# Layer-norm sums summed whole before TensorE, weight splits moved ahead of the first reads, and other orders in attention and the output projection

## The reference, cut to what matters

```
def rmsnorm(x, g):
    return x * rsqrt(mean(x * x, axis=-1) + eps) * g

def conv_ffn(x, g, w_up, conv_w, conv_b, w_down):
    u = rmsnorm(x, g) @ w_up                      # 1024 -> 2 * 2816
    c = conv_b + sum(conv_w[j] * shifted(u, j) for j in range(3))
    gate, val = split(c, 2)
    return (silu(gate) * val) @ w_down

for i in range(2):
    h = rmsnorm(x, attn_norm[i])
    y_mix = rwkv7_time_mix(...) if i == 0 else dilated_attention(q, k_sh, v_sh)
    y_mem = memory_attention(...)
    x = x + concat(y_mix, y_mem) @ w_out[i]
    x = x + conv_ffn(x, ffn_norm[i], ...)
```

## Time and profile before

| | us |
|---|---|
| time, median of 3 runs (lowest to highest) | 1308.78 (1308.62 to 1309.12) |
| the profiled execution's own time | 1308.9 |
| its span, first to last instruction | 1307.0 |
| busy: PE, DVE, ACT, POOL | 1275.2, 992.2, 646.0, 321.3 |

### The profile page before, as it was taken

How to read it: one execution, slowest core, us unless ns; L and a number is a source line. 1 busy time by engine, 2 the same in 40 slices (tenths; PEclk the granted TensorE clock), 3 DMA queues, 4 the chain that set the end, 5 groups by cost and what they waited for, 6 DMA issues and landing times.

```text
span 1307.0 us, 27113 instructions
## 1 busy us (share of the span) xinstructions
PE 1275.2 (98%) x10688; PEld 1041.3 (80%) x10688; DVE 992.2 (76%) x1486; ACT 646.0 (49%) x1068; POOL 321.3 (25%) x302
## 2 busy tenths in 40 slices
PE   7999999999999999999999999999999999999999
PEld 5876777776578888988889988776778889888898
DVE  4777777787468889857889958548578899578896
ACT  6575645563244445334546555547554453344542
POOL 3369777784420000000001256330100000000000
PEclk9999999999999999999999999999999999999999
DMA  8100111114023332233332342211133323333331
GB/s 326 49 22 32 55 55 40 55 32 168 18 97 97 96 108 90 86 104 96 96 105 90 112 143 81 65 49 33 33 98 97 96 89 122 97 96 98 119 109 46
DMA packets 30055, 114.35 MB, mean 87 GB/s; under 512 B 3456, under 2 KB 5248, under 8 KB 29184
## 3 DMA queue, kind: packets, MB, share of 16 engines
q1 hardware_dynamic: 29952, 112.89, 26.0%
HBM read 110.78 MB, written 2.10 MB: 86 GB/s over the span
## 4 chain that ended last, share of the span: by engine, by line
PE 86%; DVE 5%; ACT 3%; issue 1%; POOL 0%; DVEq 0%; POOLq 0%; ACTq 0%
PE bank L665 84%; PE bank L1384 1%; DVE arena L2132 1%; ACT arena L1581 1%; PE bank L971 0%; DVE sin_part L2696 0%; DVE cos_part L2723 0%; DVE in_lo L2143 0%; PE bank L1266 0%; DVE head_stat L2706 0%; ACT w_hi L1464 0%; DVE w_lo L2118 0%; PE bank L1289 0%; DVE stat L2210 0%; DVE cos_part L2692 0%
## 5 line engine op out<-in xcount | busy, mean ns | idle before, releaser
L665 PE MATMUL bank<-in_hi,w_hi 128*128 128x512 f32 x704 | 274.9, 390 | 0.9 <-DVE in_lo L2143 0.9
L665 PE MATMUL bank<-in_lo,w_hi 128*128 128x512 f32 x704 | 273.9, 389 | 0.0
L665 PE MATMUL bank<-in_hi,w_lo 128*128 128x512 f32 x704 | 273.9, 389 | 0.0
L1464 ACT ACTIVATE w_hi<-ring 128x1024 fp32r<-128x1024 f32 (+2 forms) x176 | 161.4, 919 | 205.2 <-PE bank L665 204.9
L665 PE MATMUL bank<-z,w_hi 128*128 128x256 f32 (+1 forms) x1088 | 221.9, 303 | 0.7 <-DVE w_lo L2118 0.7
L665 PEld LDWEIGHTS bank<-z,w_hi 128*128 128x128 f32 x1088 | 175.9, 191 | 9.7 <-DVE w_lo L2118 0.9
L2118 DVE TENSOR_TENSOR w_lo<-ring,w_hi 128x1024 fp32r<-128x1024 f32 (+2 forms) x156 | 161.1, 1035 | 26.4 <-ACT w_hi L1464 25.0
L665 PE MATMUL bank<-z,w_lo 128*128 128x256 f32 (+1 forms) x544 | 164.1, 302 | 0.0
L665 PEld LDWEIGHTS bank<-in_hi,w_hi 128*128 128x128 f32 x704 | 132.2, 188 | 29.6 <-DVE in_lo L2143 1.3
L665 PEld LDWEIGHTS bank<-in_lo,w_hi 128*128 128x128 f32 x704 | 132.2, 188 | 27.7 <-issue 0.5
L665 PEld LDWEIGHTS bank<-in_hi,w_lo 128*128 128x128 f32 x704 | 132.1, 188 | 27.4
(11 more groups left out here) (292 smaller groups left out, 2239.3 us busy)
## 6 DMA issues: line engine op xcount, KB each, us to landing
ring<-w_ring SPq DMA_DIRECT2D x119, 512.0 KB, 3.5
ring<-w_ring SPq DMA_DIRECT2D x32, 704.0 KB, 4.1
ring<-w_pairs SPq DMA_DIRECT2D x18, 512.0 KB, 3.9
arena<-w_mem SPq DMA_DIRECT2D x2, 2048.0 KB, 19.0
arena<-w_ring SPq DMA_DIRECT2D x4, 512.0 KB, 4.9
x<-xT SPq DMA_DIRECT2D x1, 2048.0 KB, 8.5
outT<-x SPq DMA_DIRECT2D x8, 256.0 KB, 2.0
mask<-masks SPq DMA_DIRECT2D x1, 1536.0 KB, 7.0
```

The lines of the kernel that those rows point to most:

```text
L665: return nc.tensor.matmul(out, lhsT, rhs, start=first, stop=last, skip_group_check=True)
L1464: return nc.scalar.activation(out, in_, ACT.Copy)
```

## The change

1. **Squares summed whole.** The sum now takes in slice 7 as well, and TensorE makes one matmul against the ones, not two. In MLP 0 POOL still adds (7 additions, not 6), and the matmul stands before slice 2 of product 1. In MLP 1 the 7 additions are DVE's, behind the split of product 1's weights, and the matmul stands before slice 7 of product 1. `squares_summed(q, n)` counts the additions.
2. **Splits ahead of reads.** In pair 0 of each MLP's first half, the split of product 3's weights stands ahead of the read of product 0 on DVE, and ahead of the first own tap on ACT.
3. **Projection of layer 1.** `turn_heads` stands one slot later in steps 9 and 13; ACT does the exponentials 6 of the memory attention ahead of the turned heads 13.
4. **Attention.** In step 0 DVE takes over one of ACT's two `pT` copies, and ACT does the exponentials 1 ahead of its other copy. In step 2 DVE's `pT` copy stands behind both halves of `masked`; in step 5 `masked` and the bound stand ahead of the normalisation. On PE, `out_b_memory(0)` stands ahead of `outputs(5)`.
5. **Output projection of layer 1.** ACT makes the high copy of attention slice 0 before it copies the last output; the weight splits stand between ACT's `in_hi` of even slices and their square.

```diff
+        def squares_summed(q, n):
+            return (0, KD - 1, 2 * KD - 3)[q] + n
...
             def square_sum(q):
-                pe.wait_ge(sem("sq_sum"), (KD - 2) * (q + 1))
-                mm(bank[7][:, :], ones, y[:, 0, :], True, False)
-                pe.wait_ge(sem("xsq"), KD * (q + 2))
-                mm(bank[7][:, :], ones, y[:, KD - 1, :], False, True).then_inc(sem("x_ss"), 1)
+                pe.wait_ge(sem("sq_sum"), squares_summed(q, KD - 1))
+                mm(bank[7][:, :], ones, y[:, 0, :]).then_inc(sem("x_ss"), 1)
...
-                            if half == 0 and q == 0 and s == 1:
-                                square_sum(2 * l)
+                            sum_at = (2, KD - 1)[l] if half == 0 and q == 0 and s == 1 else None
...
                             split_product(bank[b][:, :], n, in_hi, in_lo, KD,
+                                          between=lambda k: square_sum(2 * l) if k == sum_at else None,
...
-                if slot == 1 and 5 <= s <= 16:
+                if slot == (2 if s in (9, 13) else 1) and 5 <= s <= 16:
                     turn_heads(s - 5)
...
-            outputs(last - 2)
             pe.wait_ge(sem("da_sm"), 2 * 2 * RES)
             out_b_memory(0)
+            outputs(last - 2)
             weights(last - 1)
...
# ACT, squares()
-                    due = (slots == 1 or m % 2 == 1) and n >= N_SPLIT + 2
-                    if due:
+                    if slots == 1 and n >= N_SPLIT + 2:
                         split(n)
                     act.wait_ge(sem("x_up"), KD * e + m + 1)
                     gained_high((G_FFN0, G_FFN1)[e // 3], m, in_hi)
+                    if slots != 1 and m % 2 == 0:
+                        split(n + 1)
...
# ACT, up_pair()
+                        elif half == 0 and q == 0:
+                            split_at(p, up + 2, q)
+                            stream_root(2 * l + 1)
+                            split_at(p, up + 3, q)
+                            own_tap(0)
+                            own_tap(1)
+                            gate()
...
# ACT, step 17 of the projection, and attention
                     turned_out(12)
+                    own_exps(6)
                     turned_out(13)
-                    own_exps(6)
...
-                for b, at in ((0, 0), (1, 8 * P)):
+                for b, at in ((0, 0), (1, 8 * P))[n == 0:]:
...
+                if n == 0:
+                    exps(1)
                 weights(n)
                 if n == 0:
-                    exps(1)
                     split(N_OUTB + 1)
...
+            act.wait_ge(sem("da_y"), 2 * RES - 1)
+            operand_high(0)
             output(2 * RES - 1)
             act.wait_ge(sem("da_y"), 2 * RES)
-            for k in range(2):
-                operand_high(k)
+            operand_high(1)
...
# DVE, up_pair()
+                        if half == 0 and q == 0:
+                            split(up + 2)
+                            stream_rstd(2 * l + 1)
+                            split(up + 3)
                         for s in range(2):
-                            if half == 0 and q == 0 and s == 0:
-                                split(up + 2)
-                                stream_rstd(2 * l + 1)
                             read(s)
-                            if half or q or s:
+                            if half or q:
                                 split(2 * p + (up + 2 + s), up + 2 + s + 2 * q)
...
# DVE, attention
+                if n == 0:
+                    dve.wait_ge(sem("da_tr"), 1)
+                    V.tensor_copy(pT[:, 0, 0:T], bank[4][:, :]).then_inc(sem("da_pt"), 1)
...
-                if n >= 2:
+                if n > 2:
                     weights(n)
                 if n + 2 < 2 * RES:
+                    masked(n + 2, 1)
+                    softmax_bound(n + 2)
                     if n + 2 == 2 * RES - 1:
                         normalised(n + 1)
-                    masked(n + 2, 1)
-                    softmax_bound(n + 2)
+                if n == 2:
+                    weights(n)
...
             residual(N_OUTB, 3, 0.5)
+            for m in range(1, KD):
+                dve.wait_ge(sem("xsq"), 3 * KD + m + 1)
+                if m > 1:
+                    dve.wait_ge(sem("sq_sum"), squares_summed(2, m - 1))
+                V.tensor_tensor(y[:, 0, :], y[:, 0, :], y[:, m, :], ALU.add).then_inc(sem("sq_sum"), 1)
             mlp(1, 0)
...
# POOL
-            sum_squares(0)
-            sum_squares(1)
+            sum_squares(0, KD - 1)
+            sum_squares(1, KD - 2)
...
-            sum_squares(2)
```

More of the change, by code:

```diff
@@ L1247, in token_sums @@
             def token_sums():
-                pe.wait_ge(sem("sq_sum"), 2 * (KD - 2))
+                pe.wait_ge(sem("sq_sum"), squares_summed(1, KD - 2))
                 pe.wait_ge(sem("xsq"), 3 * KD)
@@ L1872, in up_pair @@
                                 split_at(p, up + 2 + s, q)
-                                if half == 0 and q == 0 and s == 0:
-                                    stream_root(2 * l + 1)
                                 own_tap(s)
@@ L1920, in _ @@
             mlp(0)
-            act.wait_ge(sem("sq_sum"), 2 * (KD - 2))
+            act.wait_ge(sem("sq_sum"), squares_summed(1, KD - 2))
             def group_done(g, r):
@@ L3006, in _, with sum_squares @@
                 G.tensor_tensor(out_low[k], y[:, k, :], out_high[k].bitcast(F32), ALU.subtract).then_inc(sem("y_split"), 1)
-            def sum_squares(q):
-                for m in range(1, KD - 1):
+            def sum_squares(q, last):
+                for m in range(1, last + 1):
                     pool.wait_ge(sem("xsq"), KD * (q + 1) + m + 1)
                     if m > 1:
-                        pool.wait_ge(sem("sq_sum"), (KD - 2) * q + m - 1)
+                        pool.wait_ge(sem("sq_sum"), squares_summed(q, m - 1))
                     G.tensor_tensor(y[:, 0, :], y[:, 0, :], y[:, m, :], ALU.add).then_inc(sem("sq_sum"), 1)
-            sum_squares(0)
-            sum_squares(1)
+            sum_squares(0, KD - 1)
+            sum_squares(1, KD - 2)
             pool.wait_ge(sem("w_lo"), N_PROJ + 2 - N_SPLIT)
```

## The result

| | before | changed |
|---|---|---|
| time, median (lowest to highest) | 1309.09 (1308.62 to 1309.59), 14 runs | 1311.92 (1310.52 to 1313.41), 14 runs |
| the profiled execution's own time, and its span | 1308.9, 1307.0 | 1311.66, 1309.9 |
| mean granted TensorE clock over the span | 1.000 in the profiled execution, and in all 57 runs of this kernel in the experiments | 0.996 to 0.999, never 1.000 |

The changed kernel takes 1.0021 of the time before (95% interval 1.0013 to 1.0028), 2.8 us more. The forecast was 1308.7 with an upper end of 1311.0, so it was wrong in the time and in the direction. The runs of the changed kernel also differ more among themselves than those of before, and in step with the clock: 1310.5 to 1310.6 at 0.999, 1311.7 to 1312.6 at 0.997, 1313.2 and 1313.4 at 0.996.

A forecast was written before the change was run, and what follows sets the result against it. The prediction took PE as the bound, busy 98% of the span. MLP 0 +1.1, projection -1.4 and MLP 1 +0.2 made -0.1 us, so 1308.7 us from a median 0.1 below the profiled execution; range 1305.8 to 1311.0.

The forecast's parts named there:

- MLP 1: +0.2 us, with PE having waited about 4 us: MLP 1: product 4 starts at 972.47 against 972.25 before, 0.2 us later, after PE waits for its `w_lo`.
- nearly cancel: Restarts: those of the two new waits and of the projection's three removed waits were taken to offset each other almost fully.
- third rival: Attention: its new order only moves PE's waits, G is near 0, time 1311.9 us; chance 0.13.
- G: Attention and output projection: how far PE gets ahead by the end of MLP 1's product 0, 3.2 us, bounds 0 to 5.6.
- MLP 0, +1.1: MLP 0: the early split delays product 4's `w_lo`; PE waits 2.0 us and starts product 4 1.1 us later.
- Projection, -1.4: Projection of layer 1: PE's waits on `roped` and on step 17's exponentials go, 1.4 us less, bounds 0 to 1.4.
- 0.9 us of step 17: Projection of layer 1: PE's 0.9 us wait goes, as the exponentials no longer stand behind a copy that waited for PE.
- MLP 1 by 3.4 - G: MLP 1: product 4's start changes by 3.4 us less G, so G decides one for one.
- Sum without the clock: Whole kernel: +1.1 for MLP 0, -1.4 for the projection and +0.2 for MLP 1 make -0.1 us.
- DVE's additions: MLP 1: seven additions 0.72 us apart take 5.0 us and end at 954.6, ahead of PE's 955.7.
- rival of slower additions: MLP 1: gaps of some 0.4 us between DVE's additions make root and product 4 1.7 us later, 1310.4 us; chance 0.12.
- PE stays the bound, 1302.4: Both MLPs: product 4's `w_lo` is not late, so the time falls by 6.4 us to 1302.4; chance 0.12.

The follow-up runs named there:

- first filler kernel: Changed kernel plus four float32 matmuls on constants between products 1 and 2 of MLP 1: 1310.61 us.
- parts 1 and 2 alone: Kernel before with only the squares summed whole and the splits ahead of reads: 1315.78 us.
- split back in MLP 0: Changed kernel with product 3's weight split back behind the reads in MLP 0 only, ACT's order too: 1308.69 us.
- splits back: Changed kernel with product 3's weight split back behind the reads in both MLPs, whole sums kept: 1307.08 us.
- filler in both: Changed kernel plus extra float32 matmuls on constants between products 1 and 2, four in MLP 1 and two in MLP 0: 1309.18 us.
- orders alone: Kernel before with only the new orders in projection, attention and output projection (parts 3 to 5): 1305.06 us, and 1305.68 when run again.
- without turns: Kernel before with parts 3 to 5, but without the later place of `turn_heads` in steps 9 and 13: 1305.33 us.
- whole sum early: Kernel before with parts 3 to 5, plus POOL's seven additions and one matmul ahead of product 1 in both MLPs: 1304.37 us, then 1304.40.

## Why the prediction was wrong, point by point

**The step that failed** is the term "MLP 1: +0.2 us, with PE having waited about 4 us". It priced a wait by its length and took the matmuls behind it at 0.227 us each; all that it counted for starting again was 0.50 instead of 0.39 us for the first matmul, in the sentence that the restarts "nearly cancel". Product 4's start was right within 0.1 us (972.50 against 972.47); its first 12 matmuls then took 5.29 us, not 2.72. The term is +0.2 and another +2.6 in the profiled execution. The same holds in part for MLP 0, whose wait of 1.93 us costs nothing in some executions and some 1.8 us in others (the two groups of the first filler kernel, medians 1309.08 and 1310.91; by the starts of its matmuls 1.6 us in the profiled one). None of the rivals had the clock in it, so the range had no room for it either. That the third rival, in which the attention gives nothing, came to 1311.9 us and the median is 1311.92 is coincidence: its G near 0 was measured as 3.86.

How many runs were below a clock of 1.000, by PE's longest wait on `w_lo` in the profiled execution of each kernel:

| kernels | longest wait on `w_lo`, us | runs below 1.000 |
|---|---|---|
| changed; parts 1 and 2 alone; split back in MLP 0 | 4.1 | 30 of 30 |
| splits back | 2.9 | 8 of 11 |
| filler in MLP 1 | 1.9 | 6 of 11 |
| filler in both; orders alone (twice); without turns; whole sum early (twice) | 0.7 | 0 of 42 |

The length of a wait is not all that counts, though: every kernel here, those of the last row too, has one of 1.65 us on DVE's `arena` near 107 us, among small matmuls, and the windows around it read 1.00.

The rest, by the prediction's own terms:

- **MLP 0, +1.1:** measured +1.24 (1.56 less the 0.32 that was there before). Right, and for the reason given: DVE and ACT one split later.
- **Projection, -1.4:** from product 4 of MLP 0 to the start of the attention the lag falls from 1.56 to 0.71 us, so -0.85. The 0.9 us of step 17 came; the 0.5 of the turns did not, since two new waits took its place, as the kernel without them shows.
- **G, 3.2 (too small by 0.7):** PE ends product 0 of MLP 1 at 955.79 - 21 x 0.227 = 951.02, 3.15 us before, having entered the attention 0.71 late: 3.86. The waits there fell to 1.2, 0.5, 0.3 and 0.2 us, where the earlier trace rows had 4.3 and `vtok` its 0.2. `scores(5)` waits 0.61 us, forecast some 0.5; the rival in which the attention gives nothing is out.
- **MLP 1 by 3.4 - G:** 3.4 - 3.86 = -0.46, and from +0.71 to +0.25 it is -0.46. The relation held to the digit.
- **Sum without the clock:** +1.24 - 0.85 - 0.46 = -0.1, as forecast, though the two last terms were each off by some 0.6 us and only their sum came out; and 1309.18 for the kernel with both fillers against a before of 1308.91.
- **DVE's additions:** 0.78 us apart, forecast 0.72, and PE did not wait for them. The rival of slower additions is out; by the rule on the flush in the Trainium skill (VectorE: DVE Perf Modes, "The DRAIN you can't avoid") they would be 1.11 us apart, an estimate, and the trace does not bear that out.
- **PE stays the bound, 1302.4:** out, since both waits came. What it priced can be had in part: 1304.4 with the whole sum early and the splits behind the reads.

## What to carry to other kernels

A wait that an edit adds to a busy TensorE is to be priced twice: its length, and the matmuls behind it at half the clock. Here waits of 4.1 and 1.9 us together cost 2.6 us more than their length in the median and 1.3 to 4.2 us from run to run (1310.52 to 1313.41 against 1309.18 with fillers), the 1.9 alone some 1.8 us in six runs of eleven, and runs that no longer agree with one another were the sign of it. Before trusting a mean clock of 1.000, look at the distance of matmuls behind the longest wait that the trace already has. And work that is put ahead of a chain in which each engine waits for the one before delays that chain by its whole length, while what PE gains by arriving early is spent at the next thing it waits for.

## What the runs showed of the hardware

- Behind a wait of 2.9 us the trace has 6 distances of 0.427 us between matmuls of 512 columns, behind 4.1 us it has 10, 11 and 12 (split back in MLP 0, changed kernel, parts 1 and 2 alone), then 0.23. Behind the 7.7 to 8.1 us at the kernel's start it has 5 to 13. Behind the wait of 1.93 us at the same place of the same code, two profiled executions show none (changed kernel, parts 1 and 2 alone) and another shows 7.
- Matmuls put into a wait gave back the clock and cost nothing that shows: four of float32 on constants in MLP 1 took the kernel from +2.8 to +1.5 us against the kernel before, and two more in MLP 0 to +0.3.
- The granted clock column had 1.00 at the start of the kernel where matmuls were 0.43 us apart.
- A split on DVE beside an addition on POOL took longer in MLP 0 of the changed kernel, 2.31 us where the next split took 1.23. In the kernel before, where POOL has no addition at this place, the same split took 1.22 us. PE did not wait for it in either:

```profile
386.79 0.75 DVE L2152 SCALAR_TENSOR_TENSOR in_lo<-x,par,in_hi 128x512 fp32r<-128x512 f32 x1 [1.07 <-ACT in_hi L1783]
387.46 2.31 DVE L2127 TENSOR_TENSOR w_lo<-ring,w_hi 128x1024 fp32r<-128x1024 f32 x1
391.62 1.23 DVE L2127 TENSOR_TENSOR w_lo<-ring,w_hi 128x1024 fp32r<-128x1024 f32 x1 [1.85 <-ACT w_hi L1465]
```
```profile
387.36 1.33 POOL L3034 TENSOR_TENSOR y<-y 128x512 f32<-128x512 f32 x1 [3.72 <-ACT y L1795]
```
